# w_o streamed once per half of the tokens, with the first half's norm inside the second pass

## What is computed

```python
h   = x * (1 + scale_m) + shift_m
p   = h @ w_in
A   = RWKV-7 time mixing (token shift, decay, delta-rule state)
B   = sliding-window (128) attention, 8 query heads, sinks
mix = (sigmoid(gate_a) * (A @ w_pa) + sigmoid(gate_b) * (B @ w_pb)) @ w_o
x   = LN(alpha * x + gate_m * mix)
q   = (x * (1 + scale_f) + shift_f) @ peer_wq           # 8 heads, 2 halves of 128
     # top 16 of 128 keys per half, top 16 of the 256 sums, softmax: 128 experts a token
act = gelu(einsum('bkd,bd->bk', peer_u[idx], h))
ff  = einsum('bk,bkd->bd', gate * act, peer_v[idx])
x   = LN(alpha * x + gate_f * ff)
```

## Time and profile before

| | us |
|---|---|
| runs | 4120.04, 4107.88, 4110.59 |
| median | 4110.59 |
| profiled execution | 4130.11 |
| its span, first to last instruction | 4128.3 |
| mean granted TensorE clock | 0.919 of full |
| part A: w_o, norm | 802.0 to 850.1, to 885.6 |
| part B: inputs, scan, attention | 1001 to 1328, 1582, 1694 |
| part B: merge, w_o, norm | 1765, 1770.2 to 1823.5, to 1870.3 |
| key stage, value stage | 1873 to 3038, 3040 to 4128 |

### The profile page before, as it was taken

One profiled execution on the slowest core, in us unless ns is written; L12 is line 12 of the kernel. 1 busy time (PEld: TensorE's weight loads), 2 busy tenths in 40 slices (PEclk: granted clock), 3 DMA queues, 4 the chain that ended last, 5 costly groups with the idle time before them and its releaser, 6 DMA issues.

```text
span 4128.3 us, 58553 instructions
## 1 busy us (share of the span) xinstructions
PE 3528.8 (85%) x22315; PEld 2560.1 (62%) x22315; DVE 2400.2 (58%) x4939; ACT 1136.4 (28%) x2035; POOL 1388.9 (34%) x1252
## 2 busy tenths in 40 slices
PE   6989977878988765867999999999978777999997
PEld 3777836777443663555667767777755554556786
DVE  3532242230787775773677887878646666444665
ACT  3311112232310112222226326364511111122322
POOL 0011100122025662453454453545436655553000
PEclk8999985898999895788999999999989999999999
DMA  5111151324267554858999999999999999999562
GB/s 197 62 63 48 48 214 54 126 81 132 67 213 272 165 186 144 290 177 294 328 332 336 337 340 336 359 336 359 363 332 398 389 388 386 394 390 345 171 185 79
DMA packets 382581, 1002.78 MB, mean 243 GB/s; under 512 B 36609, under 2 KB 134857, under 8 KB 374624
## 3 DMA queue, kind: packets, MB, share of 16 engines
q0 software_dynamic: 150912, 549.52, 36.3%
q1 hardware_dynamic: 231392, 449.49, 31.2%
HBM read 892.33 MB, written 106.55 MB: 242 GB/s over the span
## 4 chain that ended last, share of the span: by engine, by line
PE 33%; DMA 10%; DVE 5%; POOL 2%; issue 2%; ACT 2%; SPq 1%; DVEq 0%; ACTq 0%
PE hid_ps L3258 17%; PE kept_ps L3591 5%; PE ff_ps L2472 4%; PE score_ps L3591 4%; DMA v_raw<-in_v 3%; PE gates_ps L3268 2%; DMA v_rows<-in_v,idx_v 2%; DMA u_rows<-in_u_rows,idx_u 2%; DMA hidden_back<-hidden_saved 1%; POOL v_rows L2386 1%; DMA qt<-query_saved 1%; DVE u_rows L2413 1%; POOL u_rows L2375 1%; ACT first L3302 1%; DVE first L3330 1%
## 5 line engine op out<-in xcount | busy, mean ns | idle before, releaser
L2375 POOL DMA_INDIRECT u_rows<-in_u_rows,idx_u x512 | 619.6, 1210 | 1011.7 <-DVE dots L2413 743.3
L2386 POOL DMA_INDIRECT v_rows<-in_v,idx_v x512 | 577.3, 1127 | 428.8 <-PE ff_ps L2472 215.6
L2413 DVE CUSTOM_DVE_ANT_0 u_rows<-u_rows,x_rows 128x1024 f32<-128x1024 f32 x512 | 628.7, 1243 | 134.3 <-DMA u_rows<-in_u_rows,idx_u 83.2
L3258 PE MATMUL hid_ps<-dh,u_high 128*128 128x512 f32 x1152 | 462.1, 401 | 7.5 <-DVE u_low L3341 7.5
L3258 PE MATMUL hid_ps<-dl,u_high 128*128 128x512 f32 x1152 | 461.2, 400 | 0.0
L3258 PE MATMUL hid_ps<-dh,u_low 128*128 128x512 f32 x1152 | 460.1, 399 | 0.0
L3536 ACT ACTIVATE dh<-v_raw 128x1024 fp32r<-128x1024 f32 x128 | 135.1, 1055 | 596.1 <-DMA v_raw<-in_v 320.5
L2472 PE MATMUL ff_ps<-v_rows,diag 128*8 128x512 f32 x2048 | 250.6, 607 | 39.3 <-DMA v_rows<-in_v,idx_v 39.0
L3341 DVE TENSOR_TENSOR u_low<-u_raw,u_high 128x1024 fp32r<-128x1024 f32 x144 | 176.4, 1225 | 179.6 <-ACT u_high L3283 177.2
L3258 PEld LDWEIGHTS hid_ps<-dh,u_high 128*128 128x128 f32 x1152 | 217.6, 189 | 79.2 <-issue 21.7
L626 PE MATMUL ps_b<-hb,w_b 128*128 128x512 f32 x576 | 258.9, 603 | 7.3 <-PE ps_b L626 4.6
(11 more groups left out here) (585 smaller groups left out, 6653.7 us busy)
## 6 DMA issues: line engine op xcount, KB each, us to landing
u_raw<-in_u SPq DMA_DIRECT2D x128, 512.0 KB, 6.9
v_raw<-in_v SPq DMA_DIRECT2D x128, 512.0 KB, 6.9
hidden_saved<-hid SPq DMA_DIRECT2D x128, 256.0 KB
gates_saved<-gates SPq DMA_DIRECT2D x32, 1024.0 KB, 7.7
hidden_back<-hidden_saved SPq DMA_DIRECT2D x128, 256.0 KB, 8.5
g_back<-gates_saved SPq DMA_DIRECT2D x64, 320.0 KB
slab_late<-in_w_ada SPq DMA_DIRECT2D x16, 1024.0 KB, 7.8
g_back<-gates_saved SPq DMA_DIRECT2D x32, 384.0 KB
```

The source lines that it names most:

```text
L2375: self.nc.gpsimd.indirect_dma_start(self.u[:, n % RU], None, self.io["u_rows"], bass.IndirectOffsetOnAxis(ap=index, axis=axis)).then_inc(l ...
L2386: self.nc.gpsimd.indirect_dma_start(self.v[:, n % RV], None, self.io["v"], bass.IndirectOffsetOnAxis(ap=index, axis=0)).then_inc(self.v_la ...
L2413: V.tensor_tensor_reduce(self.u[:, n % RU], self.u[:, n % RU], self.xt[:], 1.0, 0.0, ALU.mult, ALU.add, accum_out=self.dots[:, i % 2, k:k ...
L3258: mm = nc.tensor.matmul(ps[b % 2][:], u[:, b % RING, k], h[:, k], start=at == 0, stop=at == 3 * KD - 1)
```

## The change

- **w_o.** It is streamed twice in each part, 16 steps of 24 matmuls (260 or 256 columns), the first 8 for the first half of the tokens and the next 8 for the second. That is 8 loads, 8 high parts and 8 low parts more per part. The low parts of the second pass are made by VectorE, behind the join two steps before. PSUM has four slots.
- **Norm.** The first half's mean stands behind step 9, its variance behind step 12, and its other steps between the joins of the second pass. After step 15 the second half's norm runs alone. In part A query 0 of the first half stands ahead of the second half's variance; in part B `dh` and `dl` are made by halves of the tokens.
- **Rows.** Rows 0 have a buffer of their own, `x_rows_first`; rows 1 are loaded at the start of part B.
- **Queries.** The second half of the first queries is loaded first of all at the start of part B, into the first gather buffer.
- **Exponentials.** They go to three buffers; the two copies per turn and the waits between go.
- **Merge.** The sum overwrites the first product (`whole`), and VectorE's wait for the low part moves ahead of the products.
- **Planner.** The w_o stage has room for fewer pieces. Beats behind steps 0 to 5 of the first pass hold 8 dots and two selection steps, and later ones none. Ten dots and gathers and three selection steps move into `peer_up`. Over `peer_up` the u gathers go from 189 to 193 and the v gathers from 269 to 264; in `peer_down` the last combine of gathered values moves from position 318 of 512 to 327, and eleven more gathers are left to it.

```diff
+                sparse.early_rows(sb, second)
...
+                    beside.select.on_sync(sp, io, ("query", 0, 1))
...
-                    decay = raw[p % 2][2]
-                    for e, sign in enumerate((-DECAY, DECAY, -DECAY)):
-                        act.wait_ge(scan_ready, 2 * p + (1, 1, 2)[e])
-                        if e:
-                            act.wait_ge(exp_used, 2 * p + e)
-                        S.activation(decay[:, 1:], sz, ACT.Exp, scale=sign).then_inc(exp_ready, 1)
+                    a, norm, decay = (raw[p % 2][q] for q in range(3))
+                    act.wait_ge(scan_ready, p + 1)
+                    for dst, arg, sign in ((a[:, 1:], decay[:, 1:], -DECAY), (sz, decay[:, 1:], DECAY), (norm[:, 1:], norm[:, 1:], -DECAY)):
+                        S.activation(dst, arg, ACT.Exp, scale=sign).then_inc(exp_ready, 1)
...
-                    link(V.tensor_tensor(norm[:, 1:], decay[:, 1:], sz, ALU.subtract))
-                    V.tensor_copy(sz, decay[:, 1:]).then_inc(scan_ready, 1)
+                    V.tensor_tensor(norm[:, 1:], decay[:, 1:], sz, ALU.subtract).then_inc(scan_ready, 1)
                     dve.wait_ge(exp_ready, 3 * p + 1)
-                    V.tensor_tensor(ya[:, p, 0:tp], ya[:, p, 0:tp], decay[:, 1:1 + tp], ALU.mult)
+                    V.tensor_tensor(ya[:, p, 0:tp], ya[:, p, 0:tp], a[:, 1:1 + tp], ALU.mult)
                     if part.ns:
-                        V.tensor_copy(ws[:, p], decay[:, 1 + tp:])
-                    link(V.tensor_copy(pc[:, p], decay[:, 1:1 + tp].rearrange("p (c s) -> p c s", s=C)[:, :, C - 1]))
-                    dve.sem_inc(exp_used, 1)
+                        V.tensor_copy(ws[:, p], a[:, 1 + tp:])
+                    V.tensor_copy(pc[:, p], a[:, 1:1 + tp].rearrange("p (c s) -> p c s", s=C)[:, :, C - 1])
                     dve.wait_ge(exp_ready, 3 * p + 2)
-                    V.tensor_tensor(bh[:, p, 0:tp], bh[:, p, 0:tp], decay[:, 1:1 + tp], ALU.mult)
-                    V.tensor_tensor(kh[:, p, 0:tp], kh[:, p, 0:tp], decay[:, 1:1 + tp], ALU.mult)
-                    link(V.tensor_copy(sz, norm[:, 1:]))
-                    dve.sem_inc(scan_ready, 1)
-                    dve.sem_inc(exp_used, 1)
+                    V.tensor_tensor(bh[:, p, 0:tp], bh[:, p, 0:tp], sz[:, 0:tp], ALU.mult)
+                    V.tensor_tensor(kh[:, p, 0:tp], kh[:, p, 0:tp], sz[:, 0:tp], ALU.mult)
                     dve.wait_ge(summed, place["bonus", p] + 1)
                     V.tensor_tensor(tiles(ob[:, p]), ps[place["bonus", p] % 2][:, :, 0:tn], tiles(vt[:, p]), ALU.mult)\
                         .then_inc(bonus_taken, 1)
                     dve.wait_ge(exp_ready, 3 * p + 3)
-                    link(V.tensor_tensor(kt[:, p, 0:tp], kt[:, p, 0:tp], decay[:, 1:1 + tp], ALU.mult))
+                    link(V.tensor_tensor(kt[:, p, 0:tp], kt[:, p, 0:tp], norm[:, 1:1 + tp], ALU.mult))
...
-    whole = sb(ph, f"merged_{tag}", [P, 2, tn])
+    whole = half[:, :, 0]
...
+                if n >= 2:
+                    dve.wait_ge(low, n - 1)
...
-        self.ps = [pb(ph, f"wo_ps{s}_{tag}", [P, nt, 512]) for s in range(2)]
+        self.ps = [pb(ph, f"wo_ps{s}_{tag}", [P, 2, 512]) for s in range(2)]
...
-            sp.wait_ge(self.o_low, n - 1)
-        sp.dma_start(self.raw[:, n % 2], self.io["w_o"][n]).then_inc(self.o_loaded[n % 2], 16)
+            self.low_ready(sp, n - 2)
+        sp.dma_start(self.raw[:, n % 2], self.io["w_o"][n % KD]).then_inc(self.o_loaded[n % 2], 16)
...
+    def low_ready(self, eng, n):
+        eng.wait_ge(self.o_low[n // KD], n % KD + 1)
+
+    def slot(self, n):
+        return self.ps[n // 2 % 2][:, n % 2, 0:self.size]
 
     def project(self, pe, n):
-        part = self.part
-        pe.wait_ge(self.o_low, n + 1)
-        if n >= 2:
-            pe.wait_ge(self.joined, n - 1)
-        for t, tok in enumerate(part.tiles):
-            for k in range(KD):
-                for q, (w, v) in enumerate(((self.high, self.mh), (self.high, self.ml), (self.low, self.mh))):
-                    mm = self.nc.tensor.matmul(self.ps[n % 2][:, t, 0:part.tn], w[:, n % 2, k], v[:, k, tok],
-                                               start=k == 0 and q == 0, stop=k == KD - 1 and q == 2)
+        self.low_ready(pe, n)
+        if n >= 4:
+            pe.wait_ge(self.joined, n - 3)
+        at = n // KD * self.size
+        for k in range(KD):
+            for q, (w, v) in enumerate(((self.high, self.mh), (self.high, self.ml), (self.low, self.mh))):
+                mm = self.nc.tensor.matmul(self.slot(n), w[:, n % 2, k], v[:, k, at:at + self.size],
+                                           start=k == 0 and q == 0, stop=k == KD - 1 and q == 2)
         mm.then_inc(self.o_summed, 1)
 
     def join(self, dve, n):
         V, x, part = self.nc.vector, self.x, self.part
-        src = self.ps[n % 2]
+        j, m = divmod(n, KD)
+        src = self.slot(n)
         dve.wait_ge(self.o_summed, n + 1)
-        if part.ns:
-            at = part.tn - part.ns
-            V.tensor_tensor(self.extra[:, n], src[:, part.nt - 1, at:part.tn], self.mod[:, GT_M + n, 1:], ALU.mult).then_inc(self.extra_ready, 1)
-            dve.wait_ge(self.extra_ready, n + 1)
-            V.tensor_tensor(x[:, n, part.tp:], x[:, n, part.tp:], self.extra[:, n], ALU.add).then_inc(self.extra_added, 1)
-        for t, tok in enumerate(part.tiles):
-            tok = slice(tok.start, min(tok.stop, part.tp))
-            ins = V.scalar_tensor_tensor(x[:, n, tok], src[:, t, 0:tok.stop - tok.start], self.mod[:, GT_M + n, 0:1], x[:, n, tok],
-                                         ALU.mult, ALU.add)
-        ins.then_inc(self.joined, 1)
+        size = self.size
+        if part.ns and j:
+            size -= part.ns
+            V.tensor_tensor(self.extra[:, m], src[:, size:], self.mod[:, GT_M + m, 1:], ALU.mult).then_inc(self.extra_ready, 1)
+            dve.wait_ge(self.extra_ready, m + 1)
+            V.tensor_tensor(x[:, m, part.tp:], x[:, m, part.tp:], self.extra[:, m], ALU.add).then_inc(self.extra_added, 1)
+        xt = self.tile(j)[:, m, 0:size]
+        V.scalar_tensor_tensor(xt, src[:, 0:size], self.mod[:, GT_M + m, 0:1], xt, ALU.mult, ALU.add).then_inc(self.joined, 1)
+
+    def second_pass(self, dve, n):
+
+        V = self.nc.vector
+        if KD <= n + 2 < 2 * KD:
+            self.split_low(dve, V, n + 2)
+        stage = {KD + 1: self.centre, KD + 4: self.invert, KD + 5: self.multiply, KD + 6: self.affine}.get(n)
+        if stage:
+            stage(dve, 0)
...
-                for n in range(KD):
+                for n in range(2 * KD):
                     o.project(pe, n)
-                o.mean(pe, 0)
+                    if n == KD + 1:
+                        o.mean(pe, 0)
+                    elif n == KD + 4:
+                        o.variance(pe, 0)
                 o.mean(pe, 1)
-                o.variance(pe, 0)
+                pe.wait_ge(o.joined, 2 * KD)
+                query(0, 0)
...
+                def split(j):
                     o.modulate(act, j)
                     act.wait_ge(o.modulated, (j + 1) * KD)
                     if j:
                         act.wait_ge(samples_ready, 1)
                     S.activation(sh[:, :, part.tiles[j]], hf[:, :, part.tiles[j]], ACT.Copy).then_inc(s_high, 1)
+
+                for n in range(2 * KD):
+                    o.split_high(act, n)
+                    if n == KD + 3:
+                        o.square_tile(act, 0)
+                    elif n == KD + 6:
+                        o.root(act, 0)
+                high(0)
+                high(1)
+                split(0)
+                o.square_tile(act, 1)
+                o.root(act, 1)
+                split(1)
...
-                o.centre(dve, 0)
+                    o.second_pass(dve, n)
                 o.centre(dve, 1)
-                o.scale(dve, 0)
+                low(0)
                 o.scale(dve, 1)
...
+                for n in range(ALL):
                     o.project(pe, n)
-                    if n + 1 < KD:
+                    if n + 1 < ALL:
                         beside.tensor(pe, "output", n)
-                o.mean(pe, 0)
+                    if n == KD + 1:
+                        o.mean(pe, 0)
+                    elif n == KD + 4:
+                        o.variance(pe, 0)
...
+                    if n == KD + 1:
+                        o.square_tile(act, 0)
+                    elif n == KD + 4:
+                        o.root(act, 0)
+                split(0)
                 o.square_tile(act, 1)
-                o.root(act, 0)
                 o.root(act, 1)
...
+        self.xt_first = sb(ph, "x_rows_first", [P, D])
...
-        if i:
+        if i >= 2:
             sp.wait_ge(self.dotted, i * P)
-        sp.dma_start(self.xt[:], self.io["h_rows"][i * P:(i + 1) * P]).then_inc(self.xt_loaded, 16)
+        sp.dma_start(self.rows(i), self.io["h_rows"][i * P:(i + 1) * P]).then_inc(self.xt_loaded, 16)
```

(13 more changed lines are left out.)

113 lines of the change are left out of this document (58 added, 55 removed).

## The result

The change takes 4132.44 us (median of 11 runs) against 4113.94 us before (11 runs): ratio 1.0038, with an interval from 1.0026 to 1.005. It is slower by 11 to 21 us, where a gain of 14 was forecast. Measured a second time, in another group of runs, the ratio was 1.0027 (1.0007 to 1.0047). The profiled execution has a span of 4132.4 us, only 4.1 above that of before, since the one shown before was one of the slower executions of its kernel.

What follows compares the result with a forecast made beforehand. TensorE was taken as the bound (busy 3528.8 of 4128.3 us), with waits in part B's attention and around w_o, and full DMA queues early in the value stage. Terms summed to −13.9 us: 4097 us median, range 4080 to 4114.

Steps and rivals of the forecast that it cites:

- exponentials' −1.2: Two copies per turn go; counts only after part B's last turn: −1.2 us, bounds 0 and −3.
- Early queries: Start of part B: TensorE's 5.73 us wait for the second half of the queries shrinks, −4.9 us.
- rows: Attention of part B: dots start earlier with rows loaded at part B's start, −12.5 us, bounds −17 and −6.
- w_o in part A: Streaming w_o twice: +13.0 to the last w_o matmul, −10.4 behind it, sum +2.6 us.
- query 0 of the first half starts 10 us behind: Part A, behind the last w_o matmul: join, mean 3.77, centre 2.3, low part 2.3 lead to query 0.
- w_o in part B: First pass 36 us; last w_o matmul +15.8, one half's norm behind it −19.3, sum −3.5 us.
- the w_o stream becomes the bound: Rival, chance 0.05: w_o loads land in 6.9 us, adding 28 us; total +14, 4125 us.
- Moved work: Value stage gets eleven more gathers from the w_o stage: +8 us, between 4.6 and 14.9.
- key stage's −2.4: Key stage: one combine less, 4 matmuls of 0.6 us, −2.4 us, bounds −5 and +6.
- The clock: Rival, chance 0.05: gaps drop TensorE to 1.2 GHz in both w_o first passes, +14.7 and +6.7; 4118 us.
- signs of being wrong: First-pass rounds over 9 us in A or 11 in B, clock 0.5 there, or value stage growing by 15.

Runs made afterwards that it cites:

- rows alone: The kernel before with only the rows buffer and the merge edit that makes room for it: 4104.8 us, ratio 0.9972.
- w_o once: The change without its edits to w_o and to the planner's numbers for it, w_o in one pass in both parts: 4096.45 us, 0.9954 to the kernel before.
- reordered kernel: w_o twice in part A alone, first half's affine steps moved behind the last join and query blocks' high parts made after step 7: 4098.54 us, 0.996.
- kernel with the moved work: All edits but w_o's, w_o in one pass, with the change's planner numbers: 4096.08 us, 0.995 to the kernel before.
- bare kernel with VectorE's low parts: w_o twice in part B alone, no beside work between steps, low parts on VectorE, affine steps behind the last join: 4103.55 us, 0.9978.
- both mends: In part B's bare twice-streamed w_o, all low parts on VectorE and affine steps behind the last join: 4103.55 us, 0.9978.

## Why the prediction was wrong

The stages of the table were forecast at −12.7 us together (the exponentials' −1.2 left out) and came to +10.4. Of these 23 us, 9.2 are part A, 6.5 w_o of part B, 4.2 the key stage, 2.5 the value stage and 0.7 attention.

**Early queries, exponentials, rows: right.** −4.9 and −11.8 in the profile for forecasts of −4.9 and −12.5. The exponentials show in the turns. From the first projection to the last use of an exponential in part B it was 143.8 and 144.1 us in the two kernels with the old order (before, rows alone) and 141.9 to 143.6 in the twelve profiles with the new. In part A the stage to the first scan matmul took 177.3 and 177.1 with the old, and 176.9 to 178.1 with the new: nothing, as said. All these edits together measure −19 by the ratio (w_o once; −22 by the medians), against a forecast of −18.6.

**w_o in part A: the failing step.** The sum had +13.0 to the last w_o matmul and −10.4 behind it. The first was +14.5 (62.6 instead of 48.1 us). The second was −2.7. The step that failed is "query 0 of the first half starts 10 us behind (join, mean 3.77, centre 2.3, low part 2.3)": it took VectorE as free for the last join. But when the last matmul ended, VectorE still had the end of the first half's multiply, the join before and all eight affine steps to do, partly beside POOL, ahead of the join on which everything waits. So the mean began 7.04 us behind instead of the join's 0.8, and ran cold, 6.62 us instead of 3.77. That made it 18.4, and the second half 40.7 instead of 33. The reordered kernel gives 9.7 and 32.3. So the chain was written down rightly, and the queue in front of it was left out, although the order of VectorE was known, and shown for part B.

**w_o in part B: two terms too small.** The first pass was priced at 36 us, with one gather of 0.9 us in a round, and took 41.3: four gathers stood ahead of its first new low part, single ones took up to 2.2 us, one load landed in 6.4 us instead of 4.7, and the clock fell three times (below). The passes took 72.4 us altogether, where 68.9 were forecast. Behind them it was 39.7 us to the first key matmul against 55.9, −16.2 where −19.3 was forecast: the second mean again ran cold (5.41 us), 2.3 us late, and the variance too. Both were priced at 3.8, although the first mean of before stood at 6.40 us in the row cited for this chain.

**The comparison hid the price.** The forecast set the double stream against the w_o stage of before, with 18 dots in it, and booked the dots' removal as a cost further on. The kernel with the moved work shows that their removal alone makes this stage 13.7 us shorter (109.8 to 96.1). Against that the double stream in part B costs 16.1 us in the profile. This doesn't change the sum of the forecast, but the split could not be seen to lose there. No rival of the prediction held this. The nearest was "the w_o stream becomes the bound", at 0.05: its sign was right, its mechanism was not the main one, since a load landed in 3.6 us in part A and 4.2 in part B, and not in 6.9. Single loads came near it: 6.4 us in the change, 7.0 in the bare kernel with VectorE's low parts, and there TensorE waited for it.

**Moved work: +8 against +10.5.** The key stage's −2.4 can't be seen: it took 1143.2 to 1155.9 us over all kernels, and those with the moved work lie on both sides of before. The value stage took 1094.0 to 1100.8 us where POOL has 378 operations, 1107.6 to 1111.4 where it has 389, and 1115.2 to 1118.6 where it has 398: one us per gather, where 512 KB at 386 GB/s would be 1.36.

**The clock: a rival that came true in part.** Over the whole first pass the granted clock was 0.88 in part A and 0.82 in part B, so neither ran at 1.2 GHz throughout, as the rival had it. But both began at 0.50, as before, and it fell to 0.50 again for 3.5 us in part A, after a wait of 2.46 us, and three times in part B, during the wait of 5.11 us and after those of 2.19 and 2.05 us. One of the prediction's signs of being wrong, a clock of 0.5 there, did show; the rounds, 8.5 us in part A and 10 in part B, and the value stage stayed below theirs.

```profile
799.00:830.00 31.00, 26.57 (x187) 25.94 (x188) 4.09 (x8) 7.41 (x7) 16.89 (x8) 0.88 0.46 144
817.00:820.00 3.00, 3.00 (x16) 3.00 (x16) 0.00 (x0) 0.00 (x0) 1.71 (x1) 0.50 0.83 193
862.00:881.00 19.00, 7.26 (x20) 5.58 (x20) 11.50 (x17) 7.94 (x10) 3.33 (x1) 0.66 0.16 56
1759.00:1806.00 47.00, 36.36 (x239) 35.02 (x240) 32.68 (x36) 9.54 (x9) 34.52 (x19) 0.82 0.76 246
1770.00:1773.00 3.00, 1.39 (x6) 1.40 (x7) 3.00 (x1) 0.00 (x0) 3.00 (x2) 0.50 0.90 273
1783.00:1786.00 3.00, 3.00 (x16) 3.00 (x15) 0.00 (x0) 0.00 (x0) 2.91 (x2) 0.50 0.89 298
1793.00:1796.00 3.00, 3.00 (x15) 2.74 (x14) 0.82 (x2) 0.00 (x0) 2.69 (x3) 0.51 0.84 243
1832.00:1870.00 38.00, 11.26 (x33) 8.45 (x33) 17.16 (x23) 14.45 (x20) 3.07 (x4) 0.66 0.25 87
```

In these stretches matmuls of 256 columns started 0.213 us apart instead of 0.120. For the 46 such spacings of part B that is 4.3 us of TensorE's time, an estimate of what this could cost at most.

Behind the last step the clock was 0.66 in both parts, and both second means ran cold after idle times of 7.04 and 2.29 us. That is the rule of the Trainium skill (TensorE: Matmul & The Clock Gate, "Why this matters for your kernels") at another place than the prediction looked for it. The page speaks of gaps of some length; the prediction took it for any gap. Against the forecast's terms it cost 2.9 us in part A (the mean) and 3.2 in part B (mean and variance, 5.41 each for 3.8). Against the kernel before it is less, since there too the second mean ran cold in both parts, in part A so:

```profile
857.68 5.29 PE L1968 MATMUL mean_ps_a<-x_a,consts 128*128 128x260 f32 x16 [2.50 <-DVE x_a L1973]
```

**What stays open.** In part B the gathers, the landing of single loads and the clock weren't tried apart. The scan of part B took from 174.8 to 192.6 us in the profiles, with a granted clock of 0.94 to 0.84, in kernels whose instructions there are the same up to the beside work. This is as much as the whole change, and nothing here says what sets it. The sum of the table, +10.4 (+8 with the exponentials and without the key stage), lies at or below the low end of the 11 to 21 us of the first measurement, and within the second.

## What to carry to other kernels

Before a pass is split to hide a tail behind it, write down for each engine what stands ahead of the last item that the tail waits for; work that is hidden in time but not in the queue comes out behind it. Compare a new stage with the old one under the same load of side work, not with the old one as it was. And price the second stream against what the tail can give back: here the split repaid it at best (192.8 us against 189.6 to 194.6, part A), and in part B it still cost 3.8 us after both mends.

## What the runs showed of the hardware

VectorE and POOL hold each other up when both run operations on two SBUF tensors. VectorE's multiply of 2080 columns took 4.52 and 4.53 us beside POOL's subtraction, and 2.32 without it; POOL's two took 6.87 us instead of 4.7; a dot 6.28 instead of 1.22 (and POOL's two beside it their usual 4.67), a sum of 8 columns 2.11 instead of 0.17. The rows fit turns, in which one operation waits until the other engine's is through. POOL's first low part, 2.35 us as elsewhere, would end at 858.46 + 2.35 = 860.81, and the multiply ended 2.32 us later, at 863.13; POOL's second ended at 865.33, and VectorE's sum of 8 columns at 865.35. This is read from the times and not tried by an experiment. The Trainium skill (GPSIMD Engine Reference, "Specifications") says that POOL's access to SBUF is shared with VectorE, with contention for VectorE instructions with two SBUF inputs; the traces agree. Nor did halving the columns halve a step: 24 matmuls of 256 columns took 2.88 us, as those of 260 did, and 24 of 512 took 5.44, so the sixteen half steps of part B have 46.1 us of matmuls for 43.5.
